# Gate projection last in the first mixer; one ring of PSUM banks for logits and transposed weights (five banks in the first mixer, four in the later ones)

## The chip, the cores and the metric

The kernel runs on one core of a Trainium2 chip. It is one program for five engines that run side by side and wait for each other with semaphores: PE (TensorE: matmuls and transposes, which write to the eight banks ps0 to ps7 of PSUM), DVE (VectorE), ACT (ScalarE), POOL (GpSimd) and SP, which issues the DMAs. Each engine works through its own list strictly in order. The metric is the time of one execution on the device in microseconds (us), the median of several runs.

## The reference

One first block and two second blocks, on 512 tokens of width 1024, in fp32:

```python
# first block: x -> x + mix @ w_out, then the feed-forward part
h = rms_norm(x, norm_mix[l])
proj = h @ w_in[l]
(q, kc_raw, vc_raw, ks, vs, kw, vw, gate_logits, hq, hf, hi, hg) = jnp.split(proj, split_points, axis=-1)
...
o_nsa = nsa_mixer(q, kc, vc, ks, vs.reshape(B, T, G, dh), kw, vw.reshape(B, T, G, dh), gates)
o_hgrn = hgrn2_mixer(hq, hf, hi, hg, lower_bounds[l], hgrn_o_norm[l])
mix = jnp.concatenate([o_nsa.astype(x.dtype), o_hgrn.astype(x.dtype)], axis=-1)
x = x + mix @ w_out[l]
...
# end of hgrn2_mixer: hg, the gate projection, is used here only
o = rms_norm(o, o_gain) * jax.nn.silu(hg.astype(f32)).reshape(B, T, H, dv)
```

The NSA mixer is three attentions (compressed, selected and window keys) of 8 heads over 4 blocks of 128 queries, in 2 groups of heads. The two second blocks have a stick-breaking attention (called S in the kernel) and a differential attention (D), again followed by an output projection and a feed-forward part.

## The kernel before

**The matmuls.** Each weight matrix comes in units of 128 x 1024 elements. A unit is loaded into `raw` (4 buffers), ACT copies its rounded value to `whi`, DVE writes the remainder to `wlo` (4 buffers each), and PE makes three matmuls of each product (high by high, high by low, low by high). Activations are split in the same way, hTh and hTl in the tile `hT`. A unit's buffers are free when the last matmul that reads it has ended.

**The first mixer** (`m` = 0) multiplies by `w_in` in groups named in `IN1`: hi, hf, hq, hg, cg, q, kv, four tiles (`i`) of each (three of cg) by four units (`j`), a chunk of six matmuls of 512 columns each. Chunks alternate between banks 0 and 1. As soon as hq and hf are there, the HGRN part starts (`hgrn`, four heads; `hp` steps of PE with masks by DVE, products by POOL and exponentials by ACT; `pv1` closes a head). The result of a head is normalised by DVE in the step `hn` (line 2094), which multiplies in place a tile `mixR1` that already holds silu(hg) times the gain: ACT has copied hg (`hgc`) and its sigmoid into `sqt`, and POOL has multiplied twice (`hg`, lines 2438 to 2447, the step `hgg`). So `hn` of the first head waits for all four tiles of hg. The NSA part starts when `hn` of head 3 and the last tile of kv are there (`first` in `plan_first`): for each block of queries `qi` and group `g` come logits (`nlg`, PE), maximum (`nmx`, DVE), exponential (`nex`, ACT), scaling (`psc`, POOL), transposition (`ptr`, PE), split (`pth` ACT, `ptl` DVE) and the product with the values (`npv`, PE), which accumulates in one bank per (qi, g); `fc` (ACT) and `fin` (DVE, writes `mixLT`) close a group.

**The output projection** (`gemm_out`) has 16 chunks `op` of 12 matmuls: eight of part 0 (the HGRN half, after the transpositions `mtr` of `mixR1` and their split `mTh`, `mTl` into `hT`) and eight of part 1 (the NSA half, split by `mSh` on ACT and `mSl` on POOL). `mtr` and `mSh` wait for the last chunk of the input projection (`LAST_IN`, the last of kv), since they overwrite `hT`. DVE adds each chunk to x (`xadd`). Part 0 uses bank 0 alone; the tenth chunk (`n == 9`) and all that follow wait for `fin` of the last group, as bank 1 then serves as an accumulator of `npv`. Then come the norm `f0` (square, root, scaling, transpositions `ntr` and split) and the feed-forward matmuls (`gemm_up`, `gemm_down`), which fill PE without a break.

**Rings.** A `Ring` hands its banks out in turn, and the taker waits for the release of the bank's last user. In the first mixer `tring` has banks 4 and 5 (all transpositions), `lring` banks 2, 3 and 6 (HGRN steps and logits), `oring` banks 7 and 1 (accumulators of `npv`). In the mixers 2 and 3 they are 4 and 5, 2 and 3, 6 and 7.

**The order.** Nothing is decided on the chip. A planner on the host (`Plan`, lines `plan_first` and `plan_late`) gives every step an engine, an assumed duration, what it waits for, a priority and the ring slots that it takes, and always places the step that could start first; priority decides between equal times. The times `T` that it finds order the lists of all engines (`in_time`). Chunks of the projections have the lowest priority and so fill what the mixer's steps leave. All ring sizes stand in the planner too.

Of the kernel before, what the change touches and what calls it, by code (L numbers as in the profile page):

```python
# [203 lines left out]
def decoder_program(nc, x_d, norm_mix, w_in, q_norm, k_norm, cmp_pos_k, cmp_pos_v, cmp_k_w1, cmp_k_w2,  # L204
# [143 lines left out]
    def rows(w, nk):  # L348
        for k in range(nk):
# [3 lines left out]
    IN1 = [("hi", "tok", 4, [(2328, 512)]), ("hf", "feat", 4, [(1816, 512)]), ("hq", "feat", 4, [(1304, 512)]),  # L353
           ("hg", "tok", 4, [(2840, 512)]), ("cg", "feat", 3, [(512, 256), (1280, 24)]), ("q", "tok", 4, [(0, 512)]),
           ("kv", "tok", 4, [(768, 512)])]
# [18 lines left out]
    T = {}  # L374
# [64 lines left out]
    SQ = [("hq", h) for h in range(4)] + [("hg", t) for t in range(4)] + [("q", t) for t in range(4)] + [("kv", t) for t in range(4)] + \  # L439
# [53 lines left out]
    def plan_op(P, m, fin, ring0):  # L493
        mk = "m%d" % m
        for n, (t, half, part) in enumerate([(t, half, 0) for half in range(2) for t in range(4)] + [(t, half, 1) for t in range(4) for half in range(2)]):
            unit = U["op", m, part, half]
            P.add(("op", (m, t, half, part)), "PE", 2.72, ("wlo", unit), ("wlo", unit + 1), *[("mSl" if part else "mTl", (mk, t, j)) for j in ((0, 1) if part else (2, 3))],
                  ("fin", (3, 1)) if m == 0 and n == 9 else None, seq="op", take=[(ring0 if n < 8 else "G", [("xadd", ("op", m, t, half, part))])])
# [13 lines left out]
    def plan_up(P, m):  # L512
        for part in range(2):
            for j in range(4):
                for i in range(4):
                    unit = U["up", m, 0] + j
                    P.add(("up", m, 0, part, i, j), "PE", 0.72, ("wlo", unit), *[("hTl", ("f%d" % m, t, 1)) for t in (2 * part, 2 * part + 1)], seq="gemm_up")
                    U_mm[unit] = ("up", m, 0, part, i, j)
# [14 lines left out]
    LAST_IN = {m: ("in", (m, "S1" if m else "kv", 3, 3)) for m in range(3)}  # L533

    def plan_first():
        P = Plan(T)
        P.ring("T", 2)
        P.ring("L", 3)
        P.ring("O", 2)
        P.rings["G"] = (2, [[("evV", (0, "hi", 0))], [("evV", (0, "hi", 1))]])  # L540
        P.ring("B0", 1)
# [10 lines left out]
        def sq_free(user):  # L552
            n = SQ.index(user)
            return (None if n == 0 else ("evV", (0,) + SQ[n - 1]) if SQ[n - 1][0] == "hq" else ("hgg", SQ[n - 1][1]) if SQ[n - 1][0] == "hg" else
                    ("fin", SQ[n - 1][1:]) if SQ[n - 1][0] == "fin" else ("psr", SQ[n - 1]))

        def evacs(name, i):
            k = (0, name, i)
            return [("evA", k)] if name in ("hf", "hg", "q") or (name, i) == ("cg", 2) else [("evV", k)] if name in ("hi", "hq") else [("evA", k), ("evV", k)]
        plan_in(P, 0, "n1", evacs)  # L560

        for i in range(4):
# [6 lines left out]
            P.add(("evA", (0, "hg", i)), "ACT", 2 * dA(512), last[3], sq_free(("hg", i)), pri=2)  # L569
            P.add(("hgg", i), "POOL", 2.6, ("evA", (0, "hg", i)))  # L570
# [2050 lines left out]
```

## Time and profile before

| | us |
|---|---|
| median of 3 runs (1973.38 to 1975.92) | 1974.48 |
| the profiled execution, time | 1971.68 |
| its span, from the first to the last instruction | 1970.0 |
| PE busy in the span | 1933.9 |
| DVE, ACT, POOL busy | 968.8, 790.6, 257.5 |
| HGRN steps of PE, first to last | 66.6 to 187.7 |
| NSA steps of PE, first logits to last product | 223.7 to 347.4 |
| mixer 2, mixer 3 (PE not alone in matmuls of weights) | 760 to 975, 1375 to 1580 |

Times below are microseconds from the start of the span. A matmul's duration in the profile reaches until its result has landed, while the next one starts earlier: a row with many matmuls tells the pace, and a PE that is busy all the time need not be at its pace. "Idle before <-X" is the time in which the engine did nothing before this instruction, and X is what the profile names as the last thing that it waited for. PEclk is the granted share of the PE clock (1.00 is 2.4 GHz, and 0.50 is 1.2 GHz).

### The profile page before, as it was taken

How to read it: one execution, taken by the hardware profiler on the slowest of the kernel's cores; microseconds unless marked ns; L12 is line 12 of the kernel's file. 1: busy time of each engine (PE TensorE's matmuls, PEld its weight loads, DVE VectorE, ACT ScalarE, POOL GpSimd, SP SyncE). 2: the span in 40 equal slices, each digit the busy share in tenths (PEclk: the TensorE clock that was granted, in tenths of full speed). 3: DMA queues.
4: the chain of work that ended last, by engine and by line, in shares of the span. 5: the costliest groups of instructions: out<-in, count | busy, mean ns of one | idle time of the engine just before them, and what ended most of it. 6: DMA issues, size and time to landing. Idle time of an engine off the chain costs nothing.

```text
span 1970.0 us, 24643 instructions
## 1 busy us (share of the span) xinstructions
PE 1933.9 (98%) x9842; PEld 1622.3 (82%) x9842; DVE 968.8 (49%) x1555; ACT 790.6 (40%) x1406; POOL 257.5 (13%) x334
## 2 busy tenths in 40 slices
PE   9999999999999999999999999999999899999998
PEld 7888787888888888877888888888878788888887
DVE  5546688432223357588642233337668852223334
ACT  4435566322223234377432332223547633333222
POOL 2133245000000010001011220001001102221000
PEclk9999999999999999999999999999999999999999
DMA  7211300133333322221133333332121123333331
GB/s 235 67 54 55 112 22 33 55 117 97 97 99 93 97 78 75 84 86 43 54 107 97 96 96 97 97 96 82 59 86 44 48 93 115 98 97 94 98 97 54
DMA packets 97138, 167.79 MB, mean 85 GB/s; under 512 B 8160, under 2 KB 49152, under 8 KB 97024
## 3 DMA queue, kind: packets, MB, share of 16 engines
q1 hardware_dynamic: 97024, 166.21, 27.5%
q8 instruction: 78, 1.28, 0.3%
q14 instruction: 36, 0.29, 0.0%
HBM read 164.09 MB, written 2.10 MB: 84 GB/s over the span
## 4 chain that ended last, share of the span: by engine, by line
PE 90%; DVE 5%; ACT 3%; issue 1%; DMA 0%; POOL 0%; SPq 0%; DVEq 0%; POOLq 0%; ACTq 0%
PE ps L49 86%; PE ps L52 4%; DVE wlo L71 1%; ACT sk1h L65 1%; DVE p L91 1%; DVE hTl L71 1%; ACT whi L65 0%; ACT p L62 0%; DVE x L71 0%; DVE t1l L71 0%; DVE small L82 0%; DMA raw<-in_w_in_dram 0%; DVE rot L71 0%; ACT hTh L65 0%; ACT t1h L65 0%
## 5 line engine op out<-in xcount | busy, mean ns | idle before, releaser
L65 ACT ACTIVATE whi<-raw 128x1024 fp32r<-128x1024 f32 x294 | 309.8, 1055 | 745.4 <-PE ps L49 742.5
L71 DVE TENSOR_TENSOR wlo<-raw,whi 128x1024 fp32r<-128x1024 f32 x294 | 361.3, 1230 | 417.2 <-ACT whi L65 414.5
L49 PE MATMUL ps<-hTh,whi 128*128 128x512 f32 (+1 forms) x1176 | 442.8, 377 | 0.0
L49 PE MATMUL ps<-hTh,wlo 128*128 128x512 f32 (+1 forms) x1176 | 438.0, 372 | 0.0
L49 PE MATMUL ps<-hTl,whi 128*128 128x512 f32 (+1 forms) x1176 | 437.9, 372 | 0.0
L49 PE MATMUL ps<-whi,uh 128*128 128x512 f32 x688 | 268.1, 390 | 0.0
L49 PE MATMUL ps<-whi,ul 128*128 128x512 f32 x688 | 267.8, 389 | 0.0
L49 PE MATMUL ps<-wlo,uh 128*128 128x512 f32 x688 | 267.8, 389 | 0.0
L49 PEld LDWEIGHTS ps<-hTh,wlo 128*128 128x128 f32 x1176 | 220.8, 188 | 39.6
L49 PEld LDWEIGHTS ps<-hTl,whi 128*128 128x128 f32 x1176 | 221.1, 188 | 36.9
L49 PEld LDWEIGHTS ps<-hTh,whi 128*128 128x128 f32 x1176 | 221.0, 188 | 36.6
L49 PE MATMUL ps<-whi,hTh 128*128 128x512 f32 x576 | 235.3, 409 | 3.0 <-DVE mixLT L71 1.6
L49 PE MATMUL ps<-whi,hTl 128*128 128x512 f32 x576 | 226.4, 393 | 0.0
L49 PE MATMUL ps<-wlo,hTh 128*128 128x512 f32 x576 | 225.8, 392 | 0.0
L71 DVE TENSOR_TENSOR ul<-u,uh 128x512 fp32r<-128x512 f32 x86 | 60.9, 711 | 281.2 <-ACT uh L65 281.2
L49 PEld LDWEIGHTS ps<-whi,uh 128*128 128x128 f32 x688 | 129.2, 188 | 26.8
L49 PEld LDWEIGHTS ps<-wlo,uh 128*128 128x128 f32 x688 | 129.2, 188 | 26.7
L49 PEld LDWEIGHTS ps<-whi,ul 128*128 128x128 f32 x688 | 129.2, 188 | 26.6
L49 PEld LDWEIGHTS ps<-whi,hTh 128*128 128x128 f32 x576 | 109.2, 190 | 24.3 <-DVE hTl L71 2.0
L49 PEld LDWEIGHTS ps<-whi,hTl 128*128 128x128 f32 x576 | 108.7, 189 | 23.9
L49 PEld LDWEIGHTS ps<-wlo,hTh 128*128 128x128 f32 x576 | 109.4, 190 | 19.2
L71 POOL TENSOR_TENSOR u<-gtmp 128x512 f32<-128x512 f32 x64 | 81.3, 1274 | 265.7 <-ACT gtmp L62 265.7
(232 smaller groups left out, 2156.7 us busy)
## 6 DMA issues: line engine op xcount, KB each, us to landing
raw<-in_w_ff_dram SPq DMA_DIRECT2D x128, 512.0 KB, 3.7
raw<-in_w_gate_up_dram SPq DMA_DIRECT2D x88, 256.0 KB, 3.1
raw<-in_w_in_dram SPq DMA_DIRECT2D x40, 512.0 KB, 4.5
raw<-in_w_in_dram SPq DMA_DIRECT2D x68, 256.0 KB, 3.1
raw<-in_w_down_dram SPq DMA_DIRECT2D x22, 512.0 KB, 3.6
raw<-in_w_o_dram SPq DMA_DIRECT2D x16, 512.0 KB, 3.7
x<-in_x_dram SPq DMA_DIRECT2D x8, 512.0 KB, 6.9
raw<-in_w_out_dram SPq DMA_DIRECT2D x8, 512.0 KB, 5.0
```

The costliest lines, as they stand in the source:

```text
L49: return self.eng.matmul(out, l, r, start=start, stop=stop, skip_group_check=True)
L52: return self.eng.transpose(out, in_, idn)
L65: return self.eng.activation(out, in_, ACT.Copy)
L71: return self.eng.tensor_tensor(out, a, b, op)
L91: return self.eng.tensor_tensor_scan(out, a, zero, 1.0, ALU.mult, ALU.add)
```

## The change

In the first mixer the group hg moves from the fourth to the last place. ACT writes its sigmoid to one of two new tiles `sg`, DVE multiplies it by the projection in PSUM (a new step, `evV` of hg), `hn` multiplies by the gain `hgain` instead of `mixR1`, and POOL makes one multiplication for each tile instead of two, after `hn` of the last head. `mtr` waits for `hgg` of its tile. ACT's copies of hg go away, and hg leaves the order of users of `sqt`. The tiles `sg` take the place of two buffers of `p1`, which move behind the others (five remain in the ring). `tring` and `lring` become one ring: banks 4, 5, 2, 3, 6 in the first mixer, 4, 5, 2, 3 in the later ones. `oring` of the first mixer keeps bank 7 alone. Banks 0 and 1 stay with the projections, also in `gemm_out`, and the wait for `fin` of the last group moves from the tenth chunk to the first of `gemm_up`. The norms f0, f1, f2 get a ring of their own (banks 4 and 5), which opens after the last group of the mixer and the last `mTl`. The gain of f0 is loaded after the last `plo` of kv instead of the first `op` chunk of part 1. The planner gets the same edits.

```diff
-    p1 = [r.t("p1_%d" % i, [128, 512]) for i in range(3)]
+    sg = [r.t("sg%d" % i, [128, 512]) for i in range(2)]
+    p1 = [r.t("p1_0", [128, 512])]
...
-    p1 += [r.t("p1_%d" % i, [128, 512]) for i in range(3, 6)]
+    p1 += [r.t("p1_%d" % i, [128, 512]) for i in range(1, 6)]
...
-           ("hg", "tok", 4, [(2840, 512)]), ("cg", "feat", 3, [(512, 256), (1280, 24)]), ("q", "tok", 4, [(0, 512)]),
-           ("kv", "tok", 4, [(768, 512)])]
+           ("cg", "feat", 3, [(512, 256), (1280, 24)]),
+           ("q", "tok", 4, [(0, 512)]),
+           ("kv", "tok", 4, [(768, 512)]),
+           ("hg", "tok", 4, [(2840, 512)])]
...
-        P.ring("T", 2)
-        P.ring("L", 3)
-        P.ring("O", 2)
+        P.ring("T", 5)
+        P.ring("O", 1)
...
-            P.add(("evA", (0, "hg", i)), "ACT", 2 * dA(512), last[3], sq_free(("hg", i)), pri=2)
-            P.add(("hgg", i), "POOL", 2.6, ("evA", (0, "hg", i)))
+            P.add(("evA", (0, "hg", i)), "ACT", dA(512), last[3], ("cm", (1, 3)), ("hgg", i - 2) if i >= 2 else None, pri=2)
+            P.add(("evV", (0, "hg", i)), "DVE", dV(512), ("evA", (0, "hg", i)), pri=2)
+            P.add(("hgg", i), "POOL", 1.0, ("evV", (0, "hg", i)), ("hn", 3), pri=4)
...
-                P.add(("hn", h), "DVE", 1.1, ("rs", ("hc", h)), *[("hgg", t) for t in range(4)], seq="hgrnV", pri=3)
+                P.add(("hn", h), "DVE", 1.1, ("rs", ("hc", h)), seq="hgrnV", pri=3)
...
-        plan_norm(P, fk, lambda t: [("xadd", ("op", m, t, 0, 1)), ("xadd", ("op", m, t, 1, 1))], lambda t, h: [("T", [("hTl", (fk, t, h))])])
+        P.rings["F"] = (2, [[("fS", (m, 1, 3)), ("mTl", ("m%d" % m, 3, 3))]] * 2)
+        plan_norm(P, fk, lambda t: [("xadd", ("op", m, t, 0, 1)), ("xadd", ("op", m, t, 1, 1))], lambda t, h: [("F", [("hTl", (fk, t, h))])])
...
-                b = n % 2 if m or part else 0
+                b = n % 2
                 bank_of["op", m, t, half, part] = b
                 for done in before[b]:
                     pe.wait_ge(*at(*done))
-                if m == 0 and n == 9:
-                    pe.wait_ge(*at("fin", (3, 1)))
...
+                            if j == 0 and g == 0 and m == 0:
+                                pe.wait_ge(*at("fin", (3, 1)))
...
-                        b, before = tring.take(("hTl", (key, t, half)))
+                        ring = fring
+                        if t == half == 0:
+                            ring.reset(("fS", (int(key[1]), 1, 3)) if key != "f0" else ("fin", (3, 1)), ("mTl", ("m" + key[1], 3, 3)))
+                        b, before = ring.take(("hTl", (key, t, half)))
...
-                        pe.wait_ge(*at("hn", 2 * j - 3))
+                        pe.wait_ge(*at("hgg", t))
...
-                b, before = lring.take(rel)
+                b, before = tring.take(rel)
...
-                tring.items, lring.items, oring.items = [4, 5], [2, 3], [6, 7]
-                for ring in (tring, lring, oring):
+                for ring in (tring, oring):
                     ring.reset(("hTl", ("a%d" % m, 3, 1)))
...
-                    act.copyA(mixR1[:, i, :], ps[b][:, :]).then_inc(*up("hgc", i))
-                    sq_free(("hg", i))
-                    act.act(sqt[:, :], ps[b][:, :], ACT.Sigmoid).then_inc(*up("evA", key))
+                    if i >= 2:
+                        act.wait_ge(*at("hgg", i - 2))
+                    else:
+                        act.wait_ge(*at("cm", 1))
+                    act.act(sg[i % 2][:, :], ps[b][:, :], ACT.Sigmoid).then_inc(*up("evA", key))
...
+                elif name == "hg":
+                    dve.wait_ge(*at("evA", key))
+                    dve.tt(sg[i % 2][:, :], ps[b][:, :], sg[i % 2][:, :], ALU.mult).then_inc(*up("evV", key))
...
-                    for t in range(4):
-                        dve.wait_ge(*at("hgg", t))
+                    dve.wait_ge(*at("c", "all"))
...
-                pool.wait_ge(*at("evA", (0, "hg", t)))
-                pool.wait_ge(*at("hgc", t))
-                pool.tt(mixR1[:, t, :], mixR1[:, t, :], sqt[:, :], ALU.mult).then_inc(*up("hgm", t))
-                pool.wait_ge(*at("hgm", t))
-                pool.wait_ge(*at("c", "all"))
-                m3 = mixR1[:, t, :].rearrange("p (h d) -> p h d", h=4)
-                pool.tt(m3, m3, bc(hgain[:, :], 1, [128, 4, 128]), ALU.mult).then_inc(*up("hgg", t))
+                pool.wait_ge(*at("evV", (0, "hg", t)))
+                pool.wait_ge(*at("hn", 3))
+                pool.tt(mixR1[:, t, :], mixR1[:, t, :], sg[t % 2][:, :], ALU.mult).then_inc(*up("hgg", t))
```

## Rows read from the trace of the kernel before

**Rows 1.** The page, busy time of each engine with its share of the span:

```profile
PE 1933.9 (98%) x9842; PEld 1622.3 (82%) x9842; DVE 968.8 (49%) x1555; ACT 790.6 (40%) x1406; POOL 257.5 (13%) x334
```

**Rows 2.** Busy time by stretch: length, engines busy (instructions), PEclk, DMA share, GB/s:

```profile
98.00:118.00 20.00, 20.00 (x90) 16.55 (x89) 3.00 (x3) 6.84 (x12) 8.52 (x7) 1.00 0.13 32
...
400.00:450.00 50.00, 50.00 (x222) 41.39 (x222) 13.80 (x13) 11.94 (x13) 0.00 (x0) 1.00 0.35 107
```

**Rows 3.** PE's groups by shape, 220 to 350: count, busy, mean, idle before:

```profile
L52 PE MATMUL ps<-ident,p 128*128 128x128 f32 x160 | 25.8, 280 | 0.5 <-DVE hTl L71 0.5
...
L49 PE MATMUL ps<-whi,hTh 128*128 128x512 f32 x40 | 17.0, 424 | 1.6 <-DVE mixLT L71 1.6
```

**Rows 4.** The view of busy time in steps of ten microseconds through the NSA part:

```profile
230.00:240.00 10.00, 8.19 (x37) 6.89 (x35) 4.89 (x14) 6.29 (x33) 3.56 (x4) 0.66 0.00 0
...
280.00:290.00 10.00, 10.00 (x59) 8.87 (x59) 7.69 (x17) 6.44 (x16) 3.22 (x4) 1.00 0.35 107
...
330.00:340.00 10.00, 9.31 (x63) 7.16 (x61) 8.58 (x20) 8.10 (x21) 6.08 (x7) 1.00 0.00 0
340.00:350.00 10.00, 7.13 (x43) 5.51 (x44) 4.78 (x10) 4.25 (x9) 3.10 (x4) 1.00 0.01 2
sum 130.00, PE 120.60 PEld 100.11 DVE 99.20 ACT 84.20 POOL 51.76; mean PE 9.28 PEld 7.70 DVE 7.63 ACT 6.48 POOL 3.98
```

**Rows 5.** Tiles `AT` and `kch`: duration min/median/max, first and last start:

```profile
L49 PE MATMUL ps<-hv,AT x32: 271/275/343, 89.0 to 187.5; 128*128 128x128 f32 x32
L49 PE MATMUL ps<-kch,qst x64: 262/263/263, 223.7 to 310.0; 128*128 128x32 f32 x64
```

**Rows 6.** Order of time around the first `hn`: start, duration, instruction, idle before:

```profile
114.49 2.10 DVE L71 TENSOR_TENSOR wlo<-raw,whi 128x560 fp32r<-128x560 f32 x2 [0.43 <-ACT whi L65]
...
118.12 1.38 DVE L71 TENSOR_TENSOR wlo<-raw,whi 128x560 fp32r<-128x560 f32 x1 [1.53 <-ACT whi L65]
...
118.98 1.67 POOL L71 TENSOR_TENSOR mixR<-mixR,hgain 128x512 f32<-128x512 f32 x1
...
120.79 1.13 DVE L79 SCALAR_TENSOR_TENSOR mixR<-ps,small,mixR 128x128 f32<-128x128 f32 x4 [1.29 <-POOL mixR L71]
...
121.97 1.11 PE L49 MATMUL ps<-hQ,hK 128*128 128x64 f32 x8
```

**Rows 7.** Order of time at the end of the NSA part:

```profile
348.33 0.85 DVE L71 TENSOR_TENSOR mixLT<-ps,sqt 64x256 f32<-64x256 f32 x2 [1.46 <-ACT sqt L65]
...
349.23 0.50 PE L49 MATMUL ps<-whi,hTh 128*128 128x512 f32 x1 [1.56 <-DVE mixLT L71]
...
349.70 0.74 POOL L71 TENSOR_TENSOR hTl<-mixLT,hTh 128x256 fp32r<-128x256 f32 x1 [6.80 <-ACT hTh L65]
```

**Rows 8.** The view of [rows 2], of the instructions on `whi` alone: PE, PEld, DVE, ACT:

```profile
280.00:300.00 20.00, 11.95 (x37) 6.89 (x37) 2.44 (x2) 2.11 (x2) 1.00 0.17 53
```

**Rows 9.** One border between two groups of the NSA part, DVE and PE:

```profile
277.04 0.84 DVE L71 TENSOR_TENSOR mixLT<-ps,sqt 64x256 f32<-64x256 f32 x2
```

```profile
276.54 0.47 PE L49 MATMUL ps<-t1h,vch 32*128 32x512 f32 x1
```

**Rows 10.** Durations: a new kind's nearest relatives, and the weight split:

```profile
L71 DVE TENSOR_TENSOR hq<-ps,sqt x4: 692/692/692, 65.8 to 93.5; 128x512 f32<-128x512 f32 x4
L71 POOL TENSOR_TENSOR mixR<-mixR,sqt x4: 1291/1292/1297, 101.3 to 117.6; 128x512 f32<-128x512 f32 x4
...
L71 DVE TENSOR_TENSOR wlo<-raw,whi 128x1024 fp32r<-128x1024 f32 x294 | 361.3, 1230 | 417.2 <-ACT whi L65 414.5
```

**Rows 11.** Order of time in mixer 2, around its longest stall of PE:

```profile
926.58 0.41 PE L52 MATMUL ps<-ident,mixR 128*128 128x128 f32 x2 [0.17 <-DVE hTl L71]
...
932.01 0.23 PE L49 MATMUL ps<-m_strict,identB 128*128 128x128 bf16 x1
...
935.01 0.41 DVE L71 TENSOR_TENSOR hTl<-ps,hTh 128x256 fp32r<-128x256 f32 x1
935.48 1.12 PE L52 MATMUL ps<-ident,p 128*128 128x128 f32 x4 [2.83 <-DVE hTl L71]
```

More of the change, by code:

```diff
@@ L497, in plan_op @@
             P.add(("op", (m, t, half, part)), "PE", 2.72, ("wlo", unit), ("wlo", unit + 1), *[("mSl" if part else "mTl", (mk, t, j)) for j in ((0, 1) if part else (2, 3))],
-                  ("fin", (3, 1)) if m == 0 and n == 9 else None, seq="op", take=[(ring0 if n < 8 else "G", [("xadd", ("op", m, t, half, part))])])
+                  seq="op", take=[("G", [("xadd", ("op", m, t, half, part))])])
             P.add(("xadd", ("op", m, t, half, part)), "DVE", dV(512), ("op", (m, t, half, part)), ("x", ("r", t)) if m == 0 and part == 0 else None,
@@ L516, in plan_up @@
                     unit = U["up", m, 0] + j
-                    P.add(("up", m, 0, part, i, j), "PE", 0.72, ("wlo", unit), *[("hTl", ("f%d" % m, t, 1)) for t in (2 * part, 2 * part + 1)], seq="gemm_up")
+                    P.add(("up", m, 0, part, i, j), "PE", 0.72, ("wlo", unit), *[("hTl", ("f%d" % m, t, 1)) for t in (2 * part, 2 * part + 1)],
+                          ("fin", (3, 1)) if m == 0 else None, seq="gemm_up")
                     U_mm[unit] = ("up", m, 0, part, i, j)
@@ L684, in plan_first @@
                 P.add(("fin", (qi, g)), "DVE", 0.7, ("fc", (qi, g)), seq="nfin", pri=2)
-        plan_op(P, 0, lambda kind, j, t: ("hn", 2 * j + 1) if kind == "D" else ("fin", (t, j)), "B0")
-        P.rings["B0"] = (1, [[("evV", (0, "kv", 2)), ("evA", (0, "kv", 2))]])
-        plan_norm(P, "f0", lambda t: [("xadd", ("op", 0, t, 0, 1)), ("xadd", ("op", 0, t, 1, 1))], lambda t, h: [("T", [("hTl", ("f0", t, h))])])
+        plan_op(P, 0, lambda kind, j, t: ("hgg", t) if kind == "D" else ("fin", (t, j)))
+        P.rings["F"] = (2, [[("fin", (3, 1)), ("mTl", ("m0", 3, 3))]] * 2)
+        plan_norm(P, "f0", lambda t: [("xadd", ("op", 0, t, 0, 1)), ("xadd", ("op", 0, t, 1, 1))], lambda t, h: [("F", [("hTl", ("f0", t, h))])])
         plan_up(P, 0)
@@ L1262, in nsa_logits @@
                     yield T["nlg", (it["i"], 0)]
-                    b, before = lring.take(("cad", qi))
+                    b, before = tring.take(("cad", qi))
                     for done in before:
@@ L1280, in nsa_logits @@
                     yield T["nlg", (i, r_)]
-                    b, before = lring.take(("nex", (i, r_)))
+                    b, before = tring.take(("nex", (i, r_)))
                     for done in before:
@@ L1375, in late_logits @@
                     rel = ("lex", (m, i, r_)) if it["kind"] == "D" else ("lsk", (m, i))
-                    b, before = lring.take(rel)
+                    b, before = tring.take(rel)
                     for done in before:
@@ L1422, in late_pv @@
                     n = 0
-                yield T["lpv", (m, i)]
                 for done in before:
```

68 lines of the change are left out of this document (31 added, 37 removed).

## The prediction, made before the changed kernel was seen

> **What bounds the kernel now.** First the page: PE is busy 1933.9 of 1970 us [rows 1]. That looks like nothing to win, but busy is not pace. In a feed-forward stretch 222 matmuls of 512 columns fill 50.00 us, 0.225 us each [rows 2], while each one's own duration in the NSA part is 0.42 us [rows 3], since its end is hidden under the next. Where the next has to wait, that end stands alone and still counts as busy. So I went by stretches of time and by shapes, and counted work as matmuls times pace.
>
> Through the NSA part, 220 to 350, PE is idle 130 - 120.60 = 9.4 us [rows 4]. The work in it, by the 27 groups of the view by shape (the first and the fourth stand in [rows 3]): 178 matmuls of 512 columns at 0.225 [rows 2] = 40.1; 32 of 384 at 0.17 (estimate, between the neighbours) = 5.4; 176 of 256 at 0.12 (likewise) = 21.1; 320 of 128 columns or fewer at 0.11 (eight take 1.11, one 0.28: (1.11 - 0.28) / 7 = 0.12 at most [rows 3, 6]) = 35.2; 48 bf16 masks at 0.03 (estimate) = 1.4. Sum 103.2, so **26.8 us of these 130 are lost**: 9.4 as idle time, the rest as exposed ends and in two spells of half clock. One of these lies in 230 to 240, where the clock granted is 0.66 of full, so 0.68 of the time at 1.2 GHz, with PE busy 8.19 of 10 [rows 4].
>
> Where is the loss? Where chunks of a projection stand between the NSA steps, as from 280 to 290, PE is busy 10.00 of 10 and the others wait for it; where none is left, it is busy 9.31 (330 to 340) and 7.13 (340 to 350), with DVE at 8.58 and 4.78 [rows 4]. The mixer's own chain then sets the pace. No engine but PE is full there; PE lacks **work that may run**. Outside the mixers there is next to no loss [rows 2].
>
> **The change, part by part.**
>
> *hg last.* It moves 16 chunks of 6 matmuls, 96 x 0.225 = 21.6 us, from before the NSA part into it. May NSA start earlier by that? It needs kv, which then comes 21.6 us sooner, and HGRN's end, now at 187.7 (last `AT` start 187.5 [rows 5]). HGRN has a hole today: from 98 to 118 DVE works 3.00 of 20 us [rows 2], since `hn` of head 0 waits for POOL's last product with hg, ends 118.98 + 1.67 = 120.65, runs at 120.79, and the next HGRN step of PE comes at 121.97 [rows 6]. Without that wait the hole of some 22 us closes and HGRN ends near 166. NSA then starts at 223.7 [rows 5] - 21.6 = 202, with 36 us to spare behind HGRN. By itself this earns nothing on PE, which is full in the hole too, 20.00 of 20 [rows 2]; it puts 21.6 us of filler beside the chain.
>
> *The wait for the last group.* Today seven chunks of part 1 stand behind `fin` (3, 1): PE idles 1.56 us before them [rows 7]. Now chunks of blocks 0 to 2 may run when their own groups are closed: six chunks of 12 matmuls, 72 x 0.225 = 16.2 us more filler, less the one that runs early today. What is late next: `mSh`, `mSl` of block 3, of which POOL's part takes 0.74 [rows 7]; if no chunk of block 2 is left at the end, the bubble is 1.3 us longer than today.
>
> *Together.* Filler in the part rises from 27.5 us (122 matmuls with whi or wlo, by the same view) to 27.5 + 21.6 + 16.2 = 65. Chunks run greedily, not where they would help most: beside NSA steps they take some 6 us of each 10 (from 280 to 300, by the busy time of the matmuls on `whi`, 11.95 of 20 [rows 8]). 65 us so cover 108 of the 146 us from 202 to about 348, less what the gain takes off. Loss in a covered stretch: none visible [rows 4], I take 0.3 us in 10 for exposed ends, 3. Loss in a bare one: 330 to 340 shows 0.69 idle [rows 4] and about 2.4 by the sum of shapes; 30 us of it, 7. The end bubble, 1.56 + 1.3 = 3. New loss 13, gain 26.8 - 13 = **13.8 us**. The spells of half clock are in the loss on both sides.
>
> *Costs.* One accumulator: the next group's first product now waits until `fin` of the last one has ended. Today it doesn't: at one border the product starts at 276.54 and `mixLT` ends at 277.88 [rows 9], 1.3 us; the same for all seven borders gives 0.7, 0.4, 1.3, 0.4, 0.6 and twice nothing, together 3.4. Between 0 (other steps go first) and 3.4 I take 1.5. DVE gets four products from PSUM at 0.69 and, inside the part, four weight splits of 1.23 [rows 10] and six `xadd` of about 0.69 (same shape): 2.8 + 4.9 + 4.1 = 11.8 on top of 99.2 in 130 [rows 4]. It stays below 9 in 10, where it already runs at 330 [rows 4]; I take 1 us for it. ACT loses four copies, POOL four products of 1.29 [rows 10]; the four that stay move to the end of HGRN. Moving `gbc`'s load and `p1` buffers: nothing, SP and the fifth buffer have slack. After `fin` (3, 1) only 5.4 us of chunks, not 19, cover norm f0 of the first blocks and the weight units of `gemm_up`, whose buffers come free only with the last chunks: 0 to 4 us, I take 1.
>
> *The rings.* In the first mixer a ring of five is looser for each user: HGRN's and logits' banks no longer wait for three, transpositions no longer for two. That gain is inside the 13.8, not beside it. In the mixers 2 and 3 the longest stall of PE, 2.83 us, is for a transposition's bank that was taken at 926.58 and that DVE's hTl frees at 935.42 [rows 11]. With one ring of four this bank would be wanted four takes later instead of two, and the fourth take is the logits at 932.01 [rows 11], which would then wait instead: the stall moves ahead, the owner stays DVE. So 0 for both mixers, between -3 and +3 us for each (the stall gone, or another as long).
>
> **Sum:** 13.8 - 1.5 - 1 - 1 = 10.3, about 10.5 us. 1971.68 - 10.5 = 1961.2 by the profiled execution; that lies 2.8 below the median of the runs shown, so by the median 1974.5 - 10.5 = **1964 us**.
>
> One row speaks against moving POOL's products into a stretch where DVE is full. A weight split of 560 columns beside POOL's product with hg took 1.38 us, and two others 2.10 together, so 0.33 more for one [rows 6]. Four times 0.33 is 1.3 us of DVE, inside its slack. The Trainium skill (SBUF — State Buffer, "Who interferes with whom") says that a VectorE instruction with two SBUF inputs contends with a GpSimd instruction that reads SBUF, as for an exclusive lock. By full blocking it would be 4 x 1.29 = 5.2 us of DVE instead, and if all of it lay on the path the time would be 1969; I count this in the second rival.
>
> **The rivals.**
>
> *Better.* The planner, with four banks in turn, places DVE's hTl ahead of the scans, and both late mixers lose their stall; or the bare stretch is shorter than 30 us. 2 x 2.8 and 3 more: 1953 to 1957. For: DVE is free to take hTl from 929. Against: priorities stay. Chance 0.17.
>
> *Filler used up early, or DVE full.* Greedy placing spends hg's chunks at once; `hgg` and `mtr` come late, part 0 follows, and the last block (38 us from 310 [rows 5]) stays as bare as today. Then only the front of the part gains, about 6 of its losses (in 230 to 240 alone 1.8 of idle time and 3.4 by half clock [rows 4]), less 3 of costs: 1969 to 1973. For: DVE works 8.58 of 10 in the bare stretch already. Against: chunks of part 1 are held back until each block closes, so some reach the end. Chance 0.19.
>
> *Slower.* One mechanism: taking turns in a single ring. A short user, a transposition (freed after about 1.3 us), now stands behind a long one: in the mixers 2 and 3 `skt`, `mtr` and logits. If each of the 36 items of a mixer cost 0.2 us so, that is 14 us for both, and the gain of 10.5 becomes a loss of 4: 1978 to 1984. It decides from 0.15 us per item. For: [rows 11], a bank held for 9 us. Against: a transposition's own logits were taken before it, so their bank is free by then. Chance 0.09.
>
> *It does nothing.* NSA doesn't start earlier because HGRN, with more of its steps side by side, is held by POOL or ACT to beyond 202: 1972 to 1976. Chance 0.05.
>
> **How the numbers follow.** The forecast itself, 1958 to 1969, has 0.50. Eight in ten: from 1953 (most of the better case) to 1974 (the second rival and part of the fourth). What can be told from no change is 0.2%, 4 us: 1970.5 to 1978.4. Faster: 0.50 + 0.17 + half of the second rival, 0.77. Same: the other half and the fourth, 0.14. Slower 0.09.
>
> **What would show it.** Right: AT's last start near 166 and kch's first near 202; no hole from 98 to 118; PE idle from first logits to the last chunk of `op` down from 9.4 to about 5; the feed-forward part begins some 10 us earlier, and mixers 2 and 3 take as long as before. Wrong: kch's first start above 205 (HGRN's chain was the bound); idle time before t1h,vch (one accumulator); a new wait before the first matmuls of `gemm_up` (cover gone); mixers 2 or 3 longer or shorter by over 2 us (the rings).

## The result and the profile after

The changed kernel takes 1956.3 us in the median (1954.96 to 1960.42, 4 runs), the kernel before 1974.97 beside it: ratio 0.991, 95% interval 0.9893 to 0.9927. Its profiled execution took 1957.0 us, with a span of 1955.2, 14.8 less than before. The prediction, 1964.0 with a range of 1953 to 1974, held the time and had the sign; the gain is 18.7 us by the medians and 14.7 by the two profiled executions (that of before lies 3.3 below its median), and not 10.5. So the time lies below the central forecast of 1958 to 1969 and in the stretch of the rival "better" (1953 to 1957). Of all executions only one, of the kernel of e11 below, was in a slow state (2145.6 us at a mean granted clock of 0.846), and no ratio uses it.

A mark helps to divide it: the start of the first matmul of each `gemm_down` (first, second and third block), which lies behind the mixer and the up projection of its block.

| kernel | mark 1 | mark 2 | mark 3 | 1 to 2 | 2 to 3 |
|---|---|---|---|---|---|
| before | 613.6 | 1174.7 | 1788.8 | 561.1 | 614.1 |
| after | 604.7 | 1162.9 | 1774.1 | 558.2 | 611.2 |

So 8.9 us were earned in the first mixer and 2.9 in each of the two later ones, 14.7 together.

Busy time of the engines, from the page of after:

```profile
PE 1928.5 (99%) x9842; PEld 1621.1 (83%) x9842; DVE 968.7 (50%) x1559; ACT 797.4 (41%) x1410; POOL 252.4 (13%) x330
```

DVE has four instructions more and POOL four fewer than in [rows 1], as the change says. ACT should have four fewer, 1402, since it lost four copies and nothing was added; it has 1410 instead of 1406 and is busy 6.8 us longer. So eight came that the diff doesn't name (below).

Tiles `AT` and `kch` of after, and the stretch in which HGRN had its hole (columns as in [rows 5] and [rows 2]):

```profile
L49 PE MATMUL ps<-hv,AT x32: 270/275/275, 89.1 to 163.9; 128*128 128x128 f32 x32
L49 PE MATMUL ps<-kch,qst x64: 262/263/263, 203.6 to 287.5; 128*128 128x32 f32 x64
```

```profile
98.00:118.00 20.00, 20.00 (x143) 18.52 (x142) 10.28 (x31) 8.14 (x27) 5.64 (x9) 1.00 0.05 19
```

The hole is closed (DVE 10.28 us, before 3.00) and NSA starts 20.1 us earlier. The NSA part of after in steps of ten microseconds, with the columns of [rows 4]:

```profile
202.00:212.00 10.00, 10.00 (x73) 8.69 (x71) 7.67 (x18) 6.19 (x17) 2.18 (x4) 1.00 0.51 141
...
232.00:242.00 10.00, 9.43 (x67) 8.11 (x66) 6.84 (x17) 9.02 (x23) 5.90 (x6) 1.00 0.01 2
...
272.00:282.00 10.00, 7.65 (x47) 5.90 (x45) 9.31 (x16) 9.70 (x20) 5.44 (x6) 1.00 0.36 107
282.00:292.00 10.00, 9.70 (x61) 8.50 (x60) 6.88 (x20) 5.56 (x17) 5.46 (x8) 0.83 0.16 52
...
322.00:332.00 10.00, 10.00 (x64) 8.32 (x63) 7.45 (x16) 6.53 (x15) 4.81 (x5) 1.00 0.00 0
332.00:342.00 10.00, 10.00 (x61) 8.87 (x60) 7.04 (x10) 4.29 (x7) 2.04 (x2) 1.00 0.36 107
sum 140.00, PE 136.13 PEld 114.58 DVE 104.33 ACT 95.92 POOL 56.52; mean PE 9.72 PEld 8.18 DVE 7.45 ACT 6.85 POOL 4.04
```

PE idles 3.9 us of 140, before 9.4 of 130. The end, bare in [rows 4], is full now (10.00). The weak place has moved to 272 to 282, and there not only DVE is full (9.31 of 10) but ACT too (9.70). The reason stands in ACT's order of time there:

```profile
276.28 1.28 ACT L62 ACT_TABLE_LOAD   x1
277.57 0.60 ACT L62 ACTIVATE sg<-ps 128x512 f32<-128x512 f32 x1
278.07 1.05 ACT L65 ACTIVATE whi<-raw 128x1024 fp32r<-128x1024 f32 x1
279.13 1.28 ACT L62 ACT_TABLE_LOAD   x1
280.43 0.58 ACT L62 ACTIVATE p<-ps,small 128x384 f32<-128x384 f32 x1
```

and PE's longest wait of the part follows from it:

```profile
281.15 0.66 PE L52 MATMUL ps<-ident,p 128*128 128x128 f32 x4 [1.37 <-ACT p L62]
```

Each of the four sigmoids of hg now lies between exponentials, and each needs a load of the function table before and one behind it: eight of 1.28 us, 10.3 us of ACT. In the kernel before, the sigmoids lay ahead of the NSA part.

DVE has a new delay in the same place. POOL's product of hg's last tile and a weight split of DVE run side by side:

```profile
278.98 1.27 POOL L71 TENSOR_TENSOR mixR<-mixR,sg 128x512 f32<-128x512 f32 x1 [0.76 <-DVE sg L71]
...
279.15 2.18 DVE L71 TENSOR_TENSOR wlo<-raw,whi 128x1024 fp32r<-128x1024 f32 x1
```

Such a split takes 1.22 us when POOL is idle (the median of 233 in this trace), so this one lost 0.96, most of POOL's product. Of the four products this is the only one that met a split. PE's wait before 281.15 is for ACT; what this delay costs the time isn't shown.

In mixer 2 the stall of [rows 11] (2.83) and one of 1.47 at 923.99 have given way to these two, both shorter:

```profile
913.59 1.16 PE L49 MATMUL ps<-t,vS 128*128 128x128 f32 x8 [0.42 <-DVE t L68]
...
916.58 0.41 PE L52 MATMUL ps<-ident,mixR 128*128 128x128 f32 x2 [1.84 <-DVE hTl L71]
```

**The clock in these comparisons.** Apart from one at its very end, each kernel but those of e3 and e6 shows spells of 3.4 us or a multiple of it at half clock, 1.2 GHz (PEclk 0.83 in one step of ten, as above from 282), and how many there are differs by chance too: the kernel of the first experiment has the lists of after in the first mixer, with one spell in it instead of two, and its mark 1 is 1.9 us earlier. So I also give mark 1 less half the length of all half-clock spells ahead of it ("at full clock"): before 608.5, after 601.3. That correction is an estimate; one spell costs 1.7 by it, 1.9 by that pair, and less where PE would have waited anyway (e1 below). The number of spells also depends on the kernel: the four executions of after had a mean granted clock of 0.995 to 0.997, the nine undisturbed ones of e11 0.992 to 0.994.

### The profile page after: what moved, and what is told of

It reads as the page before. It is cut to its first block, busy times and chain, and to the rows that moved or that the text cites. A ratio compares the mean times of both kernels' runs of the same rounds, so it can differ in the third digit from the quotient of the medians.

```text
span 1955.2 us, 24705 instructions
## 1 busy us (share of the span) xinstructions
PE 1928.5 (99%) x9842; PEld 1621.1 (83%) x9842; DVE 968.7 (50%) x1559; ACT 797.4 (41%) x1410; POOL 252.4 (13%) x330
## 3 DMA queue, kind: packets, MB, share of 16 engines
q8 instruction: 78, 1.28, 0.3%
## 4 chain that ended last, share of the span: by engine, by line
PE 91%; ACT 4%; DVE 4%; issue 1%; DMA 0%; POOL 0%; SPq 0%; DVEq 0%; POOLq 0%; ACTq 0%
PE ps L49 87%; PE ps L52 4%; DVE wlo L71 1%; ACT p L62 1%; ACT whi L65 1%; ACT L62 0%; ACT sk1h L65 0%; DVE hTl L71 0%; DMA raw<-in_w_in_dram 0%; DVE rot L71 0%; ACT t1h L65 0%; ACT htmB L62 0%; ACT sk0h L65 0%; DVE htmB L79 0%; DVE x L71 0%
## 5 line engine op out<-in xcount | busy, mean ns | idle before, releaser
L65 ACT ACTIVATE whi<-raw 128x1024 fp32r<-128x1024 f32 (+1 forms) x294 | 309.7, 1054 | 747.2 <-PE ps L49 744.1
L71 DVE TENSOR_TENSOR wlo<-raw,whi 128x1024 fp32r<-128x1024 f32 (+1 forms) x294 | 360.9, 1228 | 399.2 <-ACT whi L65 396.9
```

The source lines that it names most:

```text
L65: return self.eng.activation(out, in_, ACT.Copy)
L71: return self.eng.tensor_tensor(out, a, b, op)
```

## Experiments

Each is built from the kernel after unless said otherwise. The kernel before, run beside the first four, had a median of 1973.1, beside e5 to e8 1974.9 (one run), beside the last four 1972.1 and 1972.8. The kernel after was not run again beside them, so a difference to its 1956.3 is read across groups of runs in which before itself moved by 2 us; the ratios allow for that, the marks of single profiled executions do not.

### The later mixers with two rings again (e1)

```diff
-            tring.items = [4, 5, 2, 3] if m else [4, 5, 2, 3, 6]
+            tring.items = [4, 5] if m else [4, 5, 2, 3, 6]
...
-                    b, before = tring.take(rel)
+                    b, before = lring.take(rel)
```

The planner too; `lring` has banks 2 and 3.

> The changed kernel with the rings of mixers 2 and 3 split again (banks 4, 5 for transpositions, 2, 3 for logits); all else as changed. Marks are the first matmul of each down projection on whi and uh: before 613.6, 1174.7, 1788.8; after 604.7, 1162.9, 1774.1, so 8.9 us came before the first mark, 2.9 more by the second and 2.9 more by the third. Theory (the ring of four earns the 2.9 of each later mixer): first mark stays at 604.7, second goes to 1165.8, third to 1779.9, the time rises by about 6 to 1962. Rival (the 2.9 come from the norms' own ring, or from the accumulators' place in the order, which stay as changed here): all marks as after, within 1 us, time 1956 to 1957.

1961.3 us, ratio 0.9946 [0.9931, 0.9961]. Marks 602.8, 1164.3, 1778.4: from mark to mark 561.5 and 614.1, as before the change. In mixer 2 both old stalls are back in the same place of the list:

```profile
913.34 0.38 PE L49 MATMUL ps<-m_strict,identB 128*128 128x512 bf16 x1 [1.47 <-DVE sk1l L71]
...
924.83 0.81 PE L52 MATMUL ps<-ident,p 128*128 128x128 f32 x4 [2.83 <-DVE hTl L71]
```

So in mixer 2 the ring of four earns the 2.9 us. In mixer 3 the pattern is the same, but the 614.1 holds something more: before has no half-clock spell there, e1 has one at 1529, just ahead of its long stall, and the stall is a microsecond shorter than that of before. First before, then e1:

```profile
1550.97 0.66 PE L52 MATMUL ps<-ident,p 128*128 128x128 f32 x4 [2.85 <-DVE hTl L71]
```

```profile
1540.52 0.66 PE L52 MATMUL ps<-ident,p 128*128 128x128 f32 x4 [1.86 <-DVE hTl L71]
```

So up to 1.7 of the 2.9 us there (half of the spell's 3.4) may be the spell's and not the ring's.

### The first mixer: banks or filler? (e2, e7, e5)

e2 keeps hg last, but transpositions have banks 4 and 5, HGRN steps and logits 2, 3 and 6, in the planner and on the chip:

```diff
-        P.ring("T", 5)
+        P.ring("T", 2)
+        P.ring("L", 3)
...
-            tring.items = [4, 5, 2, 3] if m else [4, 5, 2, 3, 6]
+            tring.items = [4, 5, 2, 3] if m else [4, 5]
```

> The changed kernel with two rings in the first mixer (banks 4, 5 for transpositions, 2, 3, 6 for HGRN steps and logits), still one accumulator bank and hg last. Theory of the prediction (work that may run is what counts, the ring of five only lets it be used): the first mark is at 605 to 608, at most 3 us of the 8.9 lost. Rival (without the one ring the chain of the NSA part is as slow as before, and the filler is no help): first mark 610 or later, 6 us or more lost. Later mixers as changed in both.

1965.7 us, ratio 0.9955 [0.9939, 0.997]: the rival held. NSA starts at 203.6 as in after, yet mark 1 is 611.0 (at full clock 607.6): of the 8.9 us of the first mixer 2.6 are left. PE waits for the splits of transpositions, five times for 0.9 us or more, where the longest such wait of after from 202 to 342 is 0.72. The longest of e2:

```profile
274.85 0.39 PE L49 MATMUL ps<-t1h,vst 128*128 128x256 f32 x1 [2.19 <-DVE t1l L71]
```

e7 is the other half alone: the kernel before, with hg in its old place and two rings in the later mixers, and in the first mixer the ring of five, one accumulator, banks 0 and 1 for `op` and the wait moved to `gemm_up`:

```diff
-        P.ring("T", 2)
-        P.ring("L", 3)
-        P.ring("O", 2)
+        P.ring("T", 5)
+        P.ring("O", 1)
...
-                if m == 0 and n == 9:
-                    pe.wait_ge(*at("fin", (3, 1)))
```

> The kernel before with the rings of the first mixer as changed (one ring of five, one accumulator, chunks of the output projection in two banks, the wait for fin at gemm_up, the norm's own ring), but hg in fourth place with its old steps, and the later mixers as before. Two rings had cost the changed kernel 6.3 us of its 8.9 (first mark 611.0). Theory (filler and ring need each other: the ring alone can't use work that isn't there, but part 1's chunks are there): first mark 609 to 612, so 2 to 5 us of the 8.9. Rival (the ring is the change, hg last adds next to nothing): first mark 605 to 607. Later mixers as before: 561.1 and 614.1 us between the marks.

1971.3 us (one run). Mark 1 is 614.4, 0.8 later than before and outside both theories; at full clock 607.6, 0.9 earlier. Its end is bare again, with PE waiting for the last `mixLT` and then for the transpositions of the norm f0:

```profile
360.77 1.68 PE L52 MATMUL ps<-ident,htmp 128*128 128x128 f32 x8 [1.57 <-DVE mixLT L71]
```

e5 closes only HGRN's hole. It is the kernel before with the gate left out: `hn` multiplies by the gain and waits for no hg, and POOL multiplies in `sqt`, which nobody reads, so its output lacks silu(hg).

```diff
-                    for t in range(4):
-                        dve.wait_ge(*at("hgg", t))
+                    dve.wait_ge(*at("c", "all"))
```

> The kernel before, hg still in fourth place, with the multiplication of HGRN's result by silu(hg) left out: hn multiplies by the gain and waits for nothing of hg, ACT's copies of hg and one of POOL's two products go, the other is kept on a scratch tile. The result therefore lacks the gate. It closes the hole of 98 to 118 alone. Theory (the hole costs PE nothing, it only keeps NSA from starting early once hg is last): last AT start near 165 instead of 187.5, first kch start 222 to 224 as before, first mark 612 to 614 (before 613.6). Rival (the hole itself is a loss, and closing it is part of the 8.9 us): first mark 611 or earlier.

1972.1 us beside 1974.9 (one run each). The last `AT` starts at 165.5, and mark 1 is 614.1, before 613.6 (at full clock 608.9 and 608.5): the hole closed earns nothing by itself.

By mark 1 at full clock: hg last with the old rings 0.9 us, the rings with hg in its old place 0.9, both 7.2 (one accumulator and the moved wait are in all three). **Neither part alone brought the gain.** But each of these kernels also has an order of its own, and the next runs show how much an order can be worth.

### Banks or order? (e11, e12)

A ring's size acts twice: on the chip, and in the planner, which finds another order with it. e11 keeps every list of after, but takes banks on the chip as e2 does in the first mixer:

```diff
-        tring, fring, oring = Ring([4, 5, 2, 3, 6]), Ring([4, 5]), Ring([7])
+        tring, fring, oring, lring = Ring([4, 5]), Ring([4, 5]), Ring([7]), Ring([2, 3, 6])
```

> The kernel after with its lists unchanged (the planner still counts one ring of five in the first mixer, so every engine has the order of the kernel after), but on the chip the banks are split there as before: transpositions take turns in 4 and 5, HGRN steps and logits in 2, 3 and 6. It lies between the kernel after (1956.3: order and banks of one ring) and the run with two rings in both (1965.7). Theory A (the banks themselves are what the chip lacks; PE has to wait for them): 1963 to 1968, with waits of PE for transpositions' banks in 220 to 340. Theory B (what the ring of five gave was mainly another order of the lists): 1955 to 1959, no new waits over 0.7 us.

1971.9 us, ratio 0.9996 [0.9987, 1.0006]: slower than both theories said, and all of the change's gain is gone though hg is last and the later mixers keep theirs (558.2 and 614.2 from mark to mark, the second with a half-clock spell of 6.8 us that after hasn't). Mark 1 is 616.6, 11.9 later than after; at full clock 608.1, 6.8 later, and the other 5.1 are more time at half clock. PE's longest waits from 268 on:

```profile
271.33 1.04 PE L52 MATMUL ps<-ident,p 128*32 128x128 f32 x4 [2.56 <-DVE t1l L71]
...
288.02 0.69 PE L52 MATMUL ps<-ident,mixR 128*128 128x128 f32 x2 [1.95 <-DVE hTl L71]
...
291.19 1.08 PE L52 MATMUL ps<-ident,mixR 128*128 128x128 f32 x4 [1.42 <-DVE hTl L71]
```

and the stretch by busy time, where after has 9.70 of 10 for PE:

```profile
282.00:292.00 10.00, 5.54 (x31) 4.13 (x29) 6.06 (x11) 7.89 (x17) 5.68 (x8) 0.80 0.34 104
```

All three wait for the split that frees one of the two banks of transpositions. The first stands behind a weight split of 1.62 us in DVE's list (started at 269.06), the other two are turns of `mtr`. Not only `mtr` is the cause: waits of 1.68 (237.38), 0.94 (243.25) and the 2.56 above, all for transpositions of `p`, come before its first turn at 283.1. **The order of after works only with its banks.**

e12 does the reverse: banks and instructions of after, another order. The planner assumes 0.2 us more for each exponential:

```diff
-                    P.add(("nex", k), "ACT", len(hs) * (dA(N) + 0.18), ("nmx", k), seq="nex", pri=3, take=[("p1", [("ptr", (i, np_ - 1))])])
+                    P.add(("nex", k), "ACT", len(hs) * (dA(N) + 0.38), ("nmx", k), seq="nex", pri=3, take=[("p1", [("ptr", (i, np_ - 1))])])
```

> The kernel after with one number of the planner changed: each exponential of the NSA part is assumed 0.2 us longer, as the trace shows it. Same instructions, banks and waits, another order. With the gate by tanh the same edit cost 11 us, and the transpositions of hg's tiles moved from 277 to 288 forward to 261 to 273. Theory A (orders found by the planner are worth several us either way, whatever the banks): 1962 to 1968, `mixR` transposed from about 261, late waits for `mixLT` and `hTl` near 350 and 362. Theory B (the loss was peculiar to the tanh gate): 1954 to 1958.

The reason given for the edit there, and in e10, is a misreading. The trace shows 0.58 for an exponential and 0.20 for its row sums, but the two overlap each other and their neighbours; from start to start, which is what an engine's list is made of, both together take 0.56 here (kernel after):

```profile
250.24 0.58 ACT L62 ACTIVATE p<-ps,small 128x384 f32<-128x384 f32 x1
250.71 0.20 ACT L62 ACTIVATION_READ_ACCUMULATOR p<-ps,small 128x1 f32 x1
250.80 0.57 ACT L65 ACTIVATE t1h<-ps 32x512 fp32r<-32x512 f32 x1
```

The planner's 0.57 was right, and so are its values for the other widths to 0.02 us (medians of 0.34, 0.45 and 0.68 for 128, 256 and 512 columns); with the edit it thinks ACT slower than it is. As a test of another order e12 stands all the same.

1965.5 us, ratio 0.9956 [0.9939, 0.9972]. Mark 1 is 612.7 (at full clock 607.6). The misinformed planner is 9 us slower: it places hg's chunks earlier (`mixR` is transposed from 262.7 to 279.4, in after from 277.2), so the work that fills PE is spent sooner. A wait of 4.72 us comes there, the longest of PE in the NSA part of any kernel here, and ACT's order of time beside it shows two table loads, 2.6 us of it:

```profile
268.06 1.12 PE L52 MATMUL ps<-ident,p 128*128 128x128 f32 x4 [4.72 <-ACT p L62]
```

```profile
263.65 1.28 ACT L62 ACT_TABLE_LOAD   x1
264.94 0.60 ACT L62 ACTIVATE sg<-ps 128x512 f32<-128x512 f32 x1
265.43 0.59 ACT L65 ACTIVATE t1h<-ps 128x512 fp32r<-128x512 f32 x1
266.04 1.28 ACT L62 ACT_TABLE_LOAD   x1
267.34 0.58 ACT L62 ACTIVATE p<-ps,small 128x384 f32<-128x384 f32 x1
```

At the end it is bare again:

```profile
359.11 1.86 PE L52 MATMUL ps<-ident,htmp 128*128 128x128 f32 x8 [1.57 <-DVE mixLT L71]
...
370.58 0.65 PE L52 MATMUL ps<-ident,htmp 128*128 128x128 f32 x4 [1.92 <-DVE hTl L71]
```

This is the second rival of the prediction, met by another order. It also limits what e2 says: e2 has the banks and an order of its own, and an order alone is worth as much as e2 lost (9 us each). By marks at full clock they lost 6.3 each. What can be said of the banks without the order is e11. What filler alone is worth can't be taken from these runs, since hg can't be moved without a new order.

### Five banks and one accumulator, or four and two (e3)

```diff
-        P.ring("T", 5)
-        P.ring("O", 1)
+        P.ring("T", 4)
+        P.ring("O", 2)
```

On the chip `tring` has 4, 5, 2, 3 and `oring` 7, 6.

> The changed kernel with a ring of four (4, 5, 2, 3) and two accumulator banks (7, 6) in the first mixer instead of five and one. The prediction put one accumulator at 1.5 us (0 to 3.4) and the fifth bank at no price of its own. If so, the first mark comes 0 to 2 us earlier than 604.7. Rival (the fifth bank is worth more than the second accumulator): first mark 2 us or more later.

1962.8 us, ratio 0.9957 [0.994, 0.9974]; mark 1 is 610.9 with no half-clock spell ahead of it, 9.6 later than after at full clock and 2.4 later than before. In this order the second accumulator doesn't pay for the fifth bank; the end is bare again:

```profile
358.08 1.09 PE L52 MATMUL ps<-ident,htmp 128*128 128x128 f32 x8 [1.57 <-DVE mixLT L71]
...
368.80 0.65 PE L52 MATMUL ps<-ident,htmp 128*128 128x128 f32 x4 [2.76 <-DVE hTl L71]
```

With what e12 showed, how much of this is the order stays open.

### What the table loads cost (e4)

silu by tanh: with t = tanh(hg / 2), (t + 1) hg is twice silu(hg), and the norm's root takes the factor.

```diff
-                    act.act(sg[i % 2][:, :], ps[b][:, :], ACT.Sigmoid).then_inc(*up("evA", key))
+                    act.act(sg[i % 2][:, :], ps[b][:, :], ACT.Tanh, scale=0.5).then_inc(*up("evA", key))
...
-                    dve.tt(sg[i % 2][:, :], ps[b][:, :], sg[i % 2][:, :], ALU.mult).then_inc(*up("evV", key))
+                    dve.stt(sg[i % 2][:, :], sg[i % 2][:, :], cst[:, 2:3], ps[b][:, :], ALU.add, ALU.mult).then_inc(*up("evV", key))
...
-                rsqrt(cell(0, ("hc", h), 4), 1.0 / 128, ("hc", h))
+                rsqrt(cell(0, ("hc", h), 4), 4.0 / 128, ("hc", h), 4.0 * EPS)
```

> The changed kernel with the gate's sigmoid as half of one plus tanh of half the argument, in the same places of the lists; one fused DVE instruction in place of the product, and the factor of one half goes into POOL's root of the head's norm. Reason: in the trace of the changed kernel ACT loads its tables 16 times, 1.283 us each, before the change 8 times; the 8 new ones stand around the four sigmoids of hg, between exponentials. Theory: these 10.3 us of ACT lie in the NSA part, where PE still waits in 232 to 282, and cost PE 2 to 4 us: with tanh the count of loads is 8 again and the first mark comes at 601 to 603, time 1952 to 1954. Rival (ACT is busy 6.9 of 10 there and swallows them): first mark 604 to 605, time as after.

1953.0 us (1949.84 to 1954.28), ratio 0.9899 [0.9884, 0.9914]: 3.3 below after by the medians, 2.2 by the ratios, whose intervals overlap a little. It is the lowest median of the kernels with several runs. Eight table loads in all are left, and the DVE product costs 0.748 instead of 0.692:

```profile
L62 ACT ACTIVATE sg<-ps x4: 587/597/599, 214.3 to 274.1; 128x512 f32<-128x512 f32 x4
L79 DVE SCALAR_TENSOR_TENSOR sg<-sg,cst,ps x4: 747/748/748, 214.9 to 274.7; 128x512 f32<-128x512 f32 x4
```

Mark 1 is 599.6, 5.1 earlier (at full clock 597.9, 3.4 earlier). The lists of both kernels are the same, so 10.3 us of ACT, an engine that is busy 7 of 10, cost 2 to 5 us of the time. The Trainium skill (ScalarE: Activation LUTs, "What ACT_TABLE_LOAD costs") gives 1283 ns for a load and 1380 ns for a drain with it. The trace agrees on the 1.28; the drain doesn't show as idle time, after each of the eight loads around the sigmoids ACT's next instruction starts 0.01 us behind (277.57 above). The same page ("Table sets: the hidden batching unit") puts tanh in one set with exp, and this run bears it out.

### Chunks of part 1 held for the last group (e6, e9)

```diff
+                if m == 0 and n == 9:
+                    pe.wait_ge(*at("fin", (3, 1)))
```

The wait stays at `gemm_up` too; 16.2 us of filler are taken away.

> The changed kernel with the wait for the last group's fin put back at the tenth chunk of the output projection (in the planner too), so that chunks of part 1 can't run beside the last blocks of the NSA part. The prediction counted them as 16.2 us of filler in a part where it lost 2.4 us in 10 without. Theory: first mark 3 to 5 us later than 604.7, and the loss shows in 310 to 345. Rival (the filler from hg is enough, since it lasts to 277): first mark within 1.5 us of 604.7.

One run gave 1956.0, no more than after, and mark 1 at 605.1. But it had no half-clock spell ahead of it, and a new idle stretch:

```profile
340.84 0.47 PE L49 MATMUL ps<-whi,hTh 128*128 128x512 f32 x1 [1.61 <-issue]
```

So I timed the same kernel again:

> The kernel after with one step undone: in the output projection of the first mixer the tenth chunk waits for `fin` of the last group again, which takes 16.2 us of filler away from the NSA part. A single run of the same kernel gave 1955.95 with no half-clock spell before the first down projection, where the kernel after has two. Theory A (the filler of part 1 is worth something, and the single run hid it behind a luckier clock): the median is 1958 to 1960, 2 to 4 us above the kernel after. Theory B (filler at the end isn't needed, the ring of five feeds PE there): 1955 to 1957, the same as the kernel after within its spread.

1959.9 us, ratio 0.9939 [0.9919, 0.9959], 3.6 above after, although the intervals touch. Mark 1 is 607.7 (at full clock 604.3, 3.0 later than after; e6 by the same measure 3.8 later). The moved wait earns about 3 us; the single run had misled me.

### Spreading the turn from HGRN to the output (e8, e10)

`mtr` and `mSh` wait for the last chunk of hg altogether. e8, on top of e4, lets each tile wait for its own (`mSh` likewise, and both on the chip too):

```diff
-                P.add(("mtr", (m, t, j)), "PE", 0.22, fin("D", j - 2, t), LAST_IN[m], seq="mtr", pri=2, take=[("T", [("mTl", (mk, t, j))])])
+                P.add(("mtr", (m, t, j)), "PE", 0.22, fin("D", j - 2, t), LAST_IN[m] if m else ("hgg", t), seq="mtr", pri=2, take=[("T", [("mTl", (mk, t, j))])])
```

> The kernel with the gate by tanh, and each block's transpositions of mixR1 (mtr), their split and the split of mixLT wait for the hg tile of that block instead of the last chunk of hg; the same matmuls and copies. In the trace with tanh PE still loses most in 260 to 280, where hg's last tile, its product on POOL and then all eight mtr come in one burst at 274 to 284, each held by ACT and DVE. Theory: spread out, the burst's stall of 1.51 us and part of the loss go, first mark 1 to 3 us earlier than 599.6. Rival (DVE and ACT are the bound there, the work only moves): within 1 us.

1952.1 us (one run), 0.9 below e4; but mark 1 is 601.8, 2.2 later than e4 and outside both theories. The total is lower only because the later mixers ran without a half-clock spell. `mixR` is transposed from 218.1 on, and the stall of 1.51 us that e4 has at 278.87 is gone, but the filler of part 0 is spent early and the end goes bare:

```profile
347.55 1.09 PE L52 MATMUL ps<-ident,htmp 128*128 128x128 f32 x8 [1.57 <-DVE mixLT L71]
...
358.27 0.66 PE L52 MATMUL ps<-ident,htmp 128*128 128x128 f32 x4 [2.79 <-DVE hTl L71]
```

The loss moved. e10 is e4 with the planner's edit of e12, and with its misreading:

> The gate by tanh (one function table for the NSA part) and, on top, the planner's duration of each exponential raised from 0.18 to 0.38 us above its base, since the trace shows 0.58 and then 0.2 us for the row sums where 0.57 was assumed. Nothing else changes; the orders of the lists follow. Theory A (the lists are in a slightly wrong order since the planner thinks ACT faster than it is): 1949 to 1952, 1 to 4 us below the gate by tanh alone (1953.0), first matmul of the first down projection at 596 to 599. Theory B (orders only move the loss, as the earlier turn did): 1952 to 1955, mark 599 to 602.

1964.3 us, ratio 0.9948 [0.9929, 0.9968]: 11 us slower than e4 by the medians, outside both theories. Part of that is the clock: its times fall into two groups, 1957.8 and 1958.5 at a mean granted clock of 0.998, 1964.3 to 1965.5 at 0.993 and 0.994, and e4 took 1949.8 at 0.998, some 8 us less. The profiled execution is of the first group. Mark 1 is 607.5 (at full clock 605.8). As in e12, hg's tiles are transposed early (260.7 to 273.4) and the two waits at the end, 1.57 and 2.79, are there.

## Why the prediction was right, and where not

**The start of NSA: right.** 202 and 166 were said, 203.6 and 163.9 measured; the hole closed and, as said, earned nothing (e5).

**The first mixer, 10.3 us: the sum nearly right, its parts not.** Measured are 8.9 by the mark, 7.2 at full clock. That it comes near 10.3 is luck, since errors of both signs cancelled. Filler was to cover the first 108 us and leave 30 bare at the end. It went the other way. hg's four tiles were evacuated at 214.8, 235.5, 261.8 and 277.6, so their 21.6 us were spread thin over 70, and the loss lies in 232 to 292; from 302 on PE is busy 10.00 of 10. I had taken a density of 6 in 10 from [rows 8], where chunks waited in plenty, for a stretch in which they came one at a time. The term "bare stretch 7, end bubble 3" was close to nothing, and the term "covered stretch 3" was the larger one.

**The ring of five, "inside the 13.8, not beside it": the step that failed most.** I gave it no price, because no row of before showed a wait that it would remove. By e11 the new order without it loses 11.9 us at mark 1 (6.8 at full clock), the whole gain. The rows of the old order didn't show it: with two banks for transpositions PE's longest wait for a split from 220 to 340 was 0.70 us there (at 251.82), in e11 it is 2.56. A resource that looks idle must be priced in the new order. The order itself had no price either, and e12 puts one of the same size on it.

**The later mixers, 0 within 3 each: inside the bounds, the value wrong.** 2.9 each, by the ring in mixer 2 and at least in part in mixer 3 (e1); the prediction's own sign of being wrong, a change of over 2 us there, came up. I argued that the stall would pass to the logits of the fourth take; it did move ahead, to 916.58, but to the transposition of `mixR`, as 1.84 us instead of 2.83, and the 1.47 before it has gone, with one of 0.42 in its place. This half of the first rival (0.17) came true. By the profiled executions it is the whole miss: between 10.3 and 14.7 lie 4.4 us, 5.8 more here and 1.4 less in the first mixer. The rest of the 18.7 by the medians was no part of the mechanism: before was profiled in an execution 3.3 us below its median. In the nine runs of before beside e1 the time follows the mean granted clock (1970.4 at 0.996, 1975.8 at 0.992).

**ACT "loses four copies": missed.** Nobody on my list was charged for where the sigmoid stands. A function's place between others adds loads: 10.3 us of ACT, 2 to 5 us of the time (e4). The kernel before shows only one such load from 220 to 350.

**POOL beside DVE, 0.33 us for a split: mis-sized.** The "two others 2.10 together" of [rows 6] are 1.33, begun 0.72 before the end of POOL's product, and 0.74 with POOL idle, which is also what the four such splits of after take. So one of the two was held up itself. A split that begins during POOL's product waits for most of what is left of it, as the 0.96 at 279.15 shows: the price by full blocking was the right one for each meeting, but only one of the four products met a split.

**One accumulator, 1.5 us: not visible** as a wait before `t1h,vch` in after; e3, with two, was slower, though in another order. **The moved wait** was priced only within the sum; by e9 it is worth about 3. **Cover of f0, 1 us:** the one wait there is 0.62 at 370.37, and before has the same one, 0.62 at 379.23: nothing lost.

**The rivals.** Filler used up early is not what the change did, but what the same banks do under another order (e12, e10; 9 and 11 us by the medians, some 8 at equal clock). Taking turns behind a long user didn't cost anything measurable. My error bars on the first mixer should have held that: the order is the planner's, and no row of before tells which one it will find.

## What to carry to other kernels

In this kernel, banks to hold what waits and the order that a planner finds brought their gain only together; price a freed resource in the order that will run, not in the one that is traced. Before an activation is moved, look which functions lie beside it: a sigmoid between exponentials costs two table loads, and tanh can replace it. And where a greedy planner writes the lists, a change of any assumed duration is an experiment of its own, of the size of the change under study; take the durations from start to start, since the spans of a trace overlap.

## What the runs showed of the hardware

A table load takes 1.283 us on ACT, the mean of the sixteen in after, and where nothing else was to be waited for (the eight around the sigmoids) the next activation follows at once; the exponentials and tanh share a table, sigmoid doesn't (eight loads fewer in e4). An exponential of 384 columns and its row sums show spans of 0.58 and 0.20 us but take 0.56 to 0.57 from start to start. A weight split of DVE, 1.22 us alone, took 2.18 when it began 0.17 us after a POOL product of 1.27, and 1.62 in e11 when 0.54 us of a POOL product were left; a DVE instruction of 128 x 512 that reads PSUM and one tile kept its 0.68 beside such a product (after, 237.97). The half-clock spells were 3.4 to 10.2 us long, and the same stretch of code had one or two of them; so a single run can be off by some 2 us at a mark, as e6 was beside e9. In e12 the clock granted was 0.76 in the mean from 262 to 272, where PE was busy 5.28 us and idle for its one wait of 4.72; the clock was full up to 267 and fell there, near the end of that wait:

```profile
262.00:272.00 10.00, 5.28 (x30) 4.92 (x29) 6.21 (x14) 8.43 (x17) 5.16 (x6) 0.76 0.33 107
```
